# Right-hand sums of four weight quarters made in DRAM, and a new order of copies around the first relu

## The reference, cut to what matters

```python
def gmlp_mixer(h, w_in, ln_g, w_s, b_s, w_out):
    u, v = jnp.split(jax.nn.gelu(h @ w_in), 2, axis=-1)          # w_in 1024 x 4096
    v = layer_norm(v) * ln_g                                      # shortened here
    sv = jnp.einsum('gts,bnsge->bntge', tril(w_s), v) + b_s       # in chunks of 128 rows
    return (u * sv) @ w_out                                       # w_out 2048 x 1024

def channel_mlp(h, w1, w2):
    return jnp.square(jax.nn.relu(h @ w1)) @ w2                   # w1 1024 x 4096, w2 4096 x 1024

x = x + gmlp_mixer(rms_norm(x, norm1_g), ...)
x = x + channel_mlp(rms_norm(x, norm2_g), mlp_w1, mlp_w2)
return rms_norm(x, final_g)
```

## Time and profile before

| | |
|---|---|
| median of 3 runs | 1078.0 us (1076.59 to 1078.86) |
| the profiled execution, its own time | 1075.86 us |
| its span in the profile | 1073.6 us |
| PE busy | 1061.0 us (99%) |
| DVE busy | 795.4 us (74%) |
| ACT busy | 561.6 us (52%) |
| POOL busy | 43.9 us (4%) |
| transfers of SP's queue (q1) | 195.33 MB |
| transfers of POOL's queue (q0) | 9.96 MB |

### The profile page before, as it was taken

How to read it: one execution, slowest core, us unless ns; L and a number is a source line. 1 busy time by engine, 2 the same in 40 slices (tenths; PEclk the granted TensorE clock), 3 DMA queues, 4 the chain that set the end, 5 groups by cost and what they waited for, 6 DMA issues and landing times.

```text
span 1073.6 us, 13163 instructions
## 1 busy us (share of the span) xinstructions
PE 1061.0 (99%) x5050; PEld 929.5 (87%) x5050; DVE 795.4 (74%) x878; ACT 561.6 (52%) x875; POOL 43.9 (4%) x49
## 2 busy tenths in 40 slices
PE   9999999999999999999899999999999999999997
PEld 7888888888898888888788888888888888888886
DVE  5986656789789996899658548456599575777766
ACT  7864444553554434554774465454654434434456
POOL 0010000000000000111000000000000000000250
PEclk9999999999999999999999999999999999999999
DMA  9089873372875495755353734637888365343223
GB/s 337 17 188 320 230 228 113 103 249 86 323 275 220 170 349 193 198 167 158 134 180 118 229 124 172 215 108 265 323 300 341 113 236 200 118 155 121 79 79 157
DMA packets 86286, 206.39 MB, mean 192 GB/s; under 512 B 5400, under 2 KB 12592, under 8 KB 79024
## 3 DMA queue, kind: packets, MB, share of 16 engines
q1 hardware_dynamic: 82576, 195.33, 52.2%
q0 software_dynamic: 3488, 9.96, 3.8%
q10 hardware_dynamic: 160, 0.27, 0.1%
HBM read 143.67 MB, written 67.11 MB: 196 GB/s over the span
## 4 chain that ended last, share of the span: by engine, by line
PE 90%; DVE 5%; ACT 2%; issue 2%; POOL 0%; DMA 0%; DVEq 0%; ACTq 0%; POOLq 0%
PE banks L467 29%; PE banks L472 29%; PE banks L471 29%; PE banks L560 2%; PE banks L599 1%; DVE ring_low L1496 1%; DVE raw_a L1597 1%; DVE pair_low L1504 1%; DVE rows L1709 0%; DVE rows L1647 0%; ACT ring_high L1039 0%; POOL quad_a L408 0%; PE banks L567 0%; DVE rows L1474 0%; DVE raw_s L1630 0%
## 5 line engine op out<-in xcount | busy, mean ns | idle before, releaser
L1069 ACT ACTIVATE pair_high<-left_and_right 128x1024 fp32r<-128x1024 f32 x168 | 176.6, 1056 | 223.4 <-PE banks L467 186.7
L1496 DVE TENSOR_TENSOR ring_low<-left_and_right,ring_high 128x512 fp32r<-128x512 f32 x224 | 152.2, 692 | 165.4 <-ACT ring_high L1039 164.7
L1504 DVE TENSOR_TENSOR pair_low<-left_and_right,pair_high 128x1024 fp32r<-128x1024 f32 x168 | 204.2, 1232 | 85.2 <-ACT pair_high L1069 85.2
L467 PE MATMUL banks<-pair_high 128*128 128x512 f32 x672 | 255.0, 379 | 0.1
L471 PE MATMUL banks<-pair_low,pair_high 128*128 128x512 f32 x672 | 254.7, 379 | 0.0
L472 PE MATMUL banks<-pair_high,pair_low 128*128 128x512 f32 x672 | 254.7, 379 | 0.0
L1039 ACT ACTIVATE ring_high<-left_and_right 128x512 fp32r<-128x512 f32 x224 | 136.9, 627 | 219.5 <-PE banks L467 132.5
L467 PE MATMUL banks<-s_high,ring_high 128*128 128x512 f32 x384 | 146.5, 382 | 4.3 <-DVE s_low L1585 4.2
L472 PE MATMUL banks<-s_high,ring_low 128*128 128x512 f32 x384 | 146.3, 381 | 0.0
L471 PE MATMUL banks<-s_low,ring_high 128*128 128x512 f32 x384 | 146.2, 381 | 0.0
L467 PEld LDWEIGHTS banks<-pair_high 128*128 128x128 f32 x672 | 127.0, 189 | 18.4 <-DVE scratch L1694 0.5
(11 more groups left out here) (141 smaller groups left out, 1243.4 us busy)
## 6 DMA issues: line engine op xcount, KB each, us to landing
left_and_right<-sums SPq DMA_DIRECT2D x40, 1024.0 KB, 7.3
sums<-rows SPq DMA_DIRECT2D x34, 1024.0 KB, 5.2
left_and_right<-in_mlp_w_dram SPq DMA_DIRECT2D x34, 1024.0 KB, 7.2
left_and_right<-in_a_w_in_dram SPq DMA_DIRECT2D x19, 1024.0 KB, 8.4
v_blocks<-rows SPq DMA_DIRECT2D x8, 1024.0 KB, 7.9
left_and_right<-in_a_w_out_dram SPq DMA_DIRECT2D x8, 1024.0 KB, 10.5
rows<-in_x_dram SPq DMA_DIRECT2D x7, 1024.0 KB, 9.2
right_sums<-in_mlp_w_dram POOLq DMA_DIRECT2D x6, 1024.0 KB, 14.7
```

Source lines behind the costliest of these rows:

```text
L467: first = nc.tensor.matmul(ps[:, bank, :], stat_high, mov_high, start=start, stop=False, skip_group_check=True)
L1069: nc.scalar.activation(pair_high[pair_entry(d, pos, k)][:, :, :], pair_of(d, pos, k), ACT.Copy)\
L1496: nc.vector.tensor_tensor(ring_low[k][:, :], right_place(n, pos)[:, k, :], ring_high[k][:, :].bitcast(F32), ALU.subtract).then_inc(low_don ...
L1504: nc.vector.tensor_tensor(pair_low[e][:, :, :], pair_of(d, pos, k), pair_high[e][:, :, :].bitcast(F32), ALU.subtract).then_inc(low_done, 1)
```

## The change

POOL makes t1 to t4 in DRAM for n = 4, 5, 6 and 7, in one loop: each quarter's eight transfers start when the last ones of the quarter before have landed. `sum_t` is left out of DVE's stream for n = 5, 6, 7, and SP loads t1 to t4 of these quarters into the quarter buffers. For this it issues t3 and t1 ahead of the stores of the previous quarter's sums, t2 in the place of b12, and t4 in the place of the second load of b21. That makes seven loads of 1 MB for a quarter where there were five.

Around the first relu block of n = 4, ACT's stream is put in another order: `snap(4, 1)` ahead of the last two steps of s1, `high_combo(4, "s3")` and two splits of product 4 ahead of `activate(4, "c11")`. In DVE's stream `low_combo(4, "s3")` goes ahead of the splits of product 4. In quarters 2 and 3 one split of the next product (`next_low(n, 2)`) moves two operations ahead, into `gate(n, "c12")`. At the end the add of the last row block goes ahead of the scaling of the one before it.

```diff
-    return 4 * n + i + 1 + (4 if n > 4 else 0)
+    return 4 * n + i + 1
...
 def t_sum_double(d, i):
-    return (16 if d == 0 else 36 + 8 * (d - 1)) + i + 1
+    return 16 + 8 * d + i + 1
...
         scale_dram = nc.dram_tensor("row_scales", [MT, P], F32).ap()
-        t_dram = nc.dram_tensor("right_sums", [4, P, QT * NB], F32).ap()
+        t_dram = nc.dram_tensor("right_sums", [4, 4, P, QT * NB], F32).ap()
         y_dram = nc.dram_tensor("y_blocks", [4, NB, NB], F32).ap()
...
-        def t_of(t):
-            return t_dram[int(t[1]) - 1].rearrange("p (k s) -> p k s", s=NB)
+        def t_of(n, t):
+            return t_dram[n - 4, int(t[1]) - 1].rearrange("p (k s) -> p k s", s=NB)
...
-            def load_sum(t, b):
-                i = places(4)[b]
-                sp.wait_ge(t_made[t], 32)
-                load((t, 4), quarter[i][:, :, :], t_of(t), quarter_landed[i], f"quarter{i}")
+            def load_sum(n, t, b):
+                i = places(n)[b]
+                sp.wait_ge(t_made[t], 32 * (n - 3))
+                load((t, n), quarter[i][:, :, :], t_of(n, t), quarter_landed[i], f"quarter{i}")
...
                 previous_rest(prev)
+                if n > 4:
+                    sp.wait_ge(low_done, unit(n, 0, 3) + 1)
+                    load_sum(n, "t3", "b11")
+                if n >= 4:
+                    sp.wait_ge(low_done, unit(n, 1, 3) + 1)
+                    load_sum(n, "t1", "b21")
                 if prev in SUMMED:
                     store_s(prev, 0)
-                if prev in SUMMED:
                     store_s(prev, 1)
...
-                if n == 4:
-                    sp.wait_ge(low_done, unit(4, 1, 3) + 1)
-                    load_sum("t1", "b21")
                 sp.wait_ge(low_done, unit(n, 3, 3) + 1)
-                if n == 4:
-                    load_sum("t4", "b21")
+                if n >= 4:
+                    load_sum(n, "t4", "b21")
                 else:
...
                     load_weight(n + 1, "b11")
-                    if n != 4:
+                    if n < 4:
                         sp.wait_ge(t_summed, t_sum(n, 3))
-                    load_weight(n + 1, "b12")
+                        load_weight(n + 1, "b12")
+                    else:
+                        load_sum(n + 1, "t2", "b12")
                     sp.wait_ge(low_done, unit(n, 5, 3) + 1)
...
                     sp.wait_ge(low_done, unit_double(0, 6, 3) + 1)
-                    load_sum("t2", "b12")
+                    load_sum(4, "t2", "b12")
                     sp.wait_ge(low_done, unit_double(0, 6, 7) + 1)
...
                     sp.wait_ge(low_done, unit(4, 0, 3) + 1)
-                    load_sum("t3", "b11")
+                    load_sum(4, "t3", "b11")
                     sp.dma_start(y_of("c21"), block_of["c21"]).then_inc(y_stored["c21"], 16)
...
-                if n == 4 and pos in SUM_OF:
-                    act.wait_ge(*landed[SUM_OF[pos], 4])
+                if n >= 4 and pos in SUM_OF:
+                    act.wait_ge(*landed[SUM_OF[pos], n])
                 elif pos in (0, 1, 5):
...
             def right_place(n, pos):
-                return quarter[places(n)[(RIGHT_PLACE_SUMS if n == 4 else RIGHT_PLACE)[pos]]]
+                return quarter[places(n)[(RIGHT_PLACE_SUMS if n >= 4 else RIGHT_PLACE)[pos]]]
...
                     split_high(4, 3, 1)
-                    for k in range(1, 4):
-                        high_step(4, "s1", k)
+                    high_step(4, "s1", 1)
                     split_high(4, 3, 2)
+                    snap(4, 1)
+                    high_step(4, "s1", 2)
+                    high_step(4, "s1", 3)
                     split_high(4, 3, 3)
+                    high_combo(4, "s3")
+                    split_high(4, 4, 0)
+                    split_high(4, 4, 1)
                     activate(4, "c11")
...
-                if n > 0:
+                if n not in (0, 4):
                     split_high(n, 4, 0)
-                if n == 4:
-                    high_combo(4, "s3")
-                if n > 0:
                     split_high(n, 4, 1)
...
             def right_place(n, pos):
-                return quarter[places(n)[(RIGHT_PLACE_SUMS if n == 4 else RIGHT_PLACE)[pos]]]
+                return quarter[places(n)[(RIGHT_PLACE_SUMS if n >= 4 else RIGHT_PLACE)[pos]]]
...
                     args = q["b21"], q["b11"], q["b21"]
-                nc.vector.tensor_tensor(*args, ALU.subtract if n < 4 else ALU.add).then_inc(t_summed, 1)
+                nc.vector.tensor_tensor(*args, ALU.subtract).then_inc(t_summed, 1)
...
                 gate_sum(n, blk, 3)
+                if blk == "c12":
+                    next_low(n, 2)
                 gate_product(n, blk, 2)
...
                     split_low(n, 1, 0)
-                    sum_t(n, 0)
+                    if n < 4:
+                        sum_t(n, 0)
                     split_low(n, 1, 1)
...
                 if n != 4:
-                    sum_t(n, 1)
+                    if n < 4:
+                        sum_t(n, 1)
                     if n == 0:
...
                           .then_inc(drained[bank], 1)
-                if n not in (0, 4):
+                if 0 < n < 4:
                     sum_t(n, 2)
...
                     dve.wait_ge(bias_landed, 16)
+                if n == 4:
+                    low_combo(4, "s3")
                 split_low(n, 4, 0)
                 split_low(n, 4, 1)
-                if n == 4:
-                    low_combo(4, "s3")
                 if n == 0:
...
                 else:
-                    if n != 4:
+                    if n < 4:
                         sum_t(n, 3)
...
                     next_low(n, 1)
-                next_low(n, 2)
+                if kind(n) != "u":
+                    next_low(n, 2)
                 next_low(n, 3)
...
                 dve.wait_ge(o_step, m)
+                if i == 2:
+                    add_rows(2, 6, [3])
                 finish_a(m)
-                if i < 3:
+                if i < 2:
                     add_rows(2, 6, [i + 1])
...
                                     pattern=[[0, GROUPS], [-1, P]], channel_multiplier=1).then_inc(ws_masked, 1)
-            nc.gpsimd.dma_start(t_of("t1"), weight(4, "b11")).then_inc(t_made["t1"], 16)
-            nc.gpsimd.dma_start(t_of("t3"), weight(4, "b12")).then_inc(t_made["t3"], 16)
-            pool.wait_ge(t_made["t1"], 16)
-            nc.gpsimd.dma_start(t_of("t1"), weight(4, "b12"), accum_op=ALU.add).then_inc(t_made["t1"], 16)
-            pool.wait_ge(t_made["t3"], 16)
-            nc.gpsimd.dma_start(t_of("t3"), weight(4, "b22"), accum_op=ALU.add).then_inc(t_made["t3"], 16)
-            pool.wait_ge(t_made["t1"], 32)
-            nc.gpsimd.dma_start(t_of("t2"), t_of("t1")).then_inc(t_made["t2"], 16)
-            pool.wait_ge(t_made["t2"], 16)
-            nc.gpsimd.dma_start(t_of("t2"), weight(4, "b22"), accum_op=ALU.add).then_inc(t_made["t2"], 16)
-            pool.wait_ge(t_made["t2"], 32)
-            nc.gpsimd.dma_start(t_of("t4"), t_of("t2")).then_inc(t_made["t4"], 16)
-            pool.wait_ge(t_made["t4"], 16)
-            nc.gpsimd.dma_start(t_of("t4"), weight(4, "b21"), accum_op=ALU.add).then_inc(t_made["t4"], 16)
+            for n in range(4, 8):
+                before = 32 * (n - 4)
+                nc.gpsimd.dma_start(t_of(n, "t1"), weight(n, "b11")).then_inc(t_made["t1"], 16)
+                nc.gpsimd.dma_start(t_of(n, "t3"), weight(n, "b12")).then_inc(t_made["t3"], 16)
+                pool.wait_ge(t_made["t1"], before + 16)
+                nc.gpsimd.dma_start(t_of(n, "t1"), weight(n, "b12"), accum_op=ALU.add).then_inc(t_made["t1"], 16)
+                pool.wait_ge(t_made["t3"], before + 16)
+                nc.gpsimd.dma_start(t_of(n, "t3"), weight(n, "b22"), accum_op=ALU.add).then_inc(t_made["t3"], 16)
+                pool.wait_ge(t_made["t1"], before + 32)
+                nc.gpsimd.dma_start(t_of(n, "t2"), t_of(n, "t1")).then_inc(t_made["t2"], 16)
+                pool.wait_ge(t_made["t2"], before + 16)
+                nc.gpsimd.dma_start(t_of(n, "t2"), weight(n, "b22"), accum_op=ALU.add).then_inc(t_made["t2"], 16)
+                pool.wait_ge(t_made["t2"], before + 32)
+                nc.gpsimd.dma_start(t_of(n, "t4"), t_of(n, "t2")).then_inc(t_made["t4"], 16)
+                pool.wait_ge(t_made["t4"], before + 16)
+                nc.gpsimd.dma_start(t_of(n, "t4"), weight(n, "b21"), accum_op=ALU.add).then_inc(t_made["t4"], 16)
+                pool.wait_ge(t_made["t3"], before + 32)
+                pool.wait_ge(t_made["t4"], before + 32)
             y_final(pool, "c22")
...
             pool.wait_ge(low_done, unit_double(0, 5, 7) + 1)
```

## The result

The changed kernel takes 1090.37 us, the median of four runs (1089.63 to 1091.02), beside 1078.38 for four of the kernel before (1076.59 to 1078.86). The ratio is 1.0116, with a 95% interval of 1.010 to 1.0131: slower by 12 us, where +4.9 was forecast. The profiled execution took 1089.95 and its span is 1087.9, 14.3 longer than before.

A forecast was written before the change was run, and what follows sets the result against it. PE, at 99% busy, was taken to bound the kernel. Orders -5.0 and -0.5, store +4.6, loads +4.0 and clock +1.8 sum to +4.9 us: 1080.8 profiled, median 1082.9, range for 8 in 10 from 1071.5 to 1092.

The forecast's parts named there:

- What bounds the kernel: Whole kernel: PE busy 1061.0 of 1073.6 us, so only its stalls and low clock can be won; DVE's sums worth 0.
- The new order at n = 4: First relu block of n = 4: stall and low clock go, 6.0 us, less 1.0 for later steps; gain 5.0.
- The end: Last row block: its add starts about 0.5 us earlier, ahead of the previous block's scaling; gain 0.5, at most 0.75.
- POOL's transfers: Quarters 1 to 3: three more sets end between 290 and 352 us, one under way at 211 and at 267 to 287.
- The load of v's c22: Quarters 2 and 3: load 4.3 us late with 2.3 in hand; PE stalls 2.0 in each, 4.0 together.
- The store ahead of `snap(3, 1)` in quarter 3: SP's store lands 7 us late, bound 22, against a 2.4 margin at the small matmuls; PE stalls 4.6, clock adds 1.8.
- The sum: Whole kernel: -5.0 - 0.5 + 4.6 + 4.0 + 1.8 = +4.9 us; 1080.8 for the profiled execution, 1082.9 as median.
- the likeliest case: Whole kernel: the forecast itself, a slower kernel, chance 0.47, own range 1080.2 to 1090 us.
- Rival 3: Quarters 2 and 3: SP's queue backs up worse, store 15 us late, 12.6 of stall, 3 per load; 1094.7, chance 0.08.
- Rival 4: n = 4: the new order does not take the stall away, 5 us dearer than forecast; 1087.9, chance 0.05.
- 1: Rival, quarters 2 and 3: transfers hidden, stores under 2.4 us late and loads under 2.3; -5.5 remains, 1072.5, chance 0.29.
- 2: Rival, whole kernel: gains and losses cancel, stalls with their clock cost of 3.3 to 7.7 us; 1078, chance 0.11.

The follow-up runs named there:

- experiment 7: Changed kernel with the set for n = 5 straight behind n = 4, and n = 6 and 7 in quarters 4 and 5: 1071.12 us, ratio 0.995.
- experiment 1: Kernel before plus only the new orders and the moved split, without the sets for n = 5 to 7; DVE keeps its sums: 1070.26 us, ratio 0.9942.
- experiment 6: Changed kernel with the set for n = 5 moved to the first double, n = 6 and 7 to quarters 4 and 5: 1096.59 us, ratio 1.0178.
- experiment 2: Kernel before plus three further POOL sets behind that for n = 4, results unused: 1094.92 us, ratio 1.0172.
- experiment 4: Kernel before plus one unused POOL set held back to about 261 us: 1090.22 us, ratio 1.0125.
- experiment 5: As experiment 4, with the set's four adding transfers made plain copies of the same size: 1088.23 us, ratio 1.0106.
- experiment 8: Experiment 1 with `snap(4, 1)` behind the split of s3 and two splits of product 4, y's c21 squares behind the split of s4: 1070.54 us, ratio 0.9943.
- experiment 10: Experiment 8 run once more unchanged, against the kernel before: 1069.43 us, ratio 0.9926.

## Why the prediction was right in its sign and wrong in its size

- **What bounds the kernel.** Right: PE's standing still and its clock set the time, and DVE's 25 us off cost or gave nothing that shows (experiment 7 against 1).
- **The new order at n = 4.** -5.0 forecast, -5.4 measured in the changed kernel: the stall -4.4, the clock -1.8, the third step of s1 +0.54 for 0.5, product 5 +0.24 for 0.5. Right in each part.
- **The end.** -0.5 forecast, -0.39 measured.
- **POOL's transfers.** The sets end at 329.7, inside 290 to 352, and are under way at the places named. Right.
- **The load of v's c22.** Quarter 2: 2.0 forecast, 1.15 + 0.99 = 2.1 measured. Quarter 3: 2.0 forecast, 0.3 measured. In quarter 3 the load, issued at 317.33, landed in 7.6 us, 2.8 later than the 4.8 of before and not 4.3: POOL's queue had nothing to move until its last add, issued at 318.58, and had moved 0.5 MB when the load landed.
- **The store ahead of `snap(3, 1)` in quarter 3: this is the step that failed, and by its size.** I had written "less than half of the bound, and I take 7"; it was 12.9, and the bound of 22 held. I had argued that a set does not always move data, and that what is lost early is partly won back. Up to the store's issue it was not: 2.46 of the 4.19 MB in front of it were still to be moved, where before none were. SP's queue did get the engines to itself, but from 294.2 to 301.6 only, when the store had been waiting for 6 us. So it landed in 17.5 us for 5.5. The margin was off too: PE does not wait at the small matmuls (2.4) but earlier, at the banks of product 4 (1.8), which the same copy empties. Stall and clock came to 11.0 + 2.0 = 13.0 for 4.6 + 1.8 = 6.4.
- **A term left out:** the load of v's c21 for quarter 3, for which ACT waited 0.84 before. It came 9.5 late with nearly 7 in hand, and cost 2.7. Small steps that no term covers come to 1.6 (0.17, 0.62, 0.83).
- **The sum.** Forecast: +4.9. Measured in the profiled execution +14.1: 6.6 more for the store, 2.7 for c21, 1.6 small steps, -1.5 for c22, -0.3 for the orders and the end, which is 9.1 of the 9.2 between them. The medians differ by 12.0 and not 14.1; the executions of one kernel lie 1.4 us (experiment 1) to 8.5 us (experiment 6) apart. The median of 1090.37 is inside the range for 8 in 10 (1071.5 to 1092) and just above the likeliest case's own (1080.2 to 1090).
- **The rivals.** Rival 3 (the store late by 15, 1094.7) had the right mechanism and came nearer to the truth than the forecast in the stall, 12.6 for 11.0; at 0.08 it had too little. Rival 4 did not occur, and neither did 1 and 2: the transfers were not hidden, and they cost far more than the orders gained.

What stays open is how late the store would have been without the backlog in front of it, beside POOL's transfers alone. It was not tried with the store issued on another queue.

## What to carry to other kernels

Traffic that no engine waits for is not free: here it took its turns on the DMA engines, and its price was set by the loads and stores with the least margin in the stretch where it ran. Before it is placed, list for each transfer there how long its landing is ahead of its use, those without a wait too, and count a queue's backlog, not each transfer alone; then place it where the list is long. With one engine at 99%, taking work off another bought nothing here, and reordering one split ahead of a relu bought more than twelve operations removed.

## What the runs showed of the hardware that was not expected

- The store of 1 MB from SP took 5.5 us to land with POOL's queue idle, 13.6 beside the set of plain copies and 16.5 beside the set with adds, in both with a backlog of SP's own queue in front of it. Turns went by packets and not by bytes: 260 to 261 packets were 0.53 to 0.52 MB beside adds, 269 to 267 were 0.55 to 1.06 beside copies.
- POOL's copy from one place of `right_sums` to another went in sixteen packets of 64 KB, which took 2.4 us each by the trace. In the changed kernel they stood from 291.4 to 295.7, and in 292.5:294 SP's queue started only ten packets (0.02 MB).
- After a stall the clock's lower level cost PE between 1.6 and 3.1 us, not in step with the stall's length: 1.6 behind a wait of 2.35 (experiment 2), 1.8 behind the stall of 4.2 before and 2.9 behind the same one in experiment 4, 2.65 behind 6.2 (experiment 5), 2.8 behind 9.2 (experiment 4), 3.1 behind 9.4 (experiment 2), 2.0 behind 11.0. A short stall did not always bring it. Behind the wait at the small matmuls of c21, 2.35 us in experiment 2 and 2.40 in the changed kernel, the granted clock was 0.50 in the one and 1.00 in the other:
```profile
256.90:259.00 2.10, 2.08 (x9) 2.08 (x10) 1.58 (x2) 2.10 (x5) 0.00 (x0) 0.50 1.08 201
...
257.00:259.00 2.00, 1.98 (x17) 1.98 (x18) 1.48 (x2) 2.00 (x5) 0.00 (x0) 1.00 1.03 159
```
- Beside the one set that every version has, for n = 4, quarter 1 was longer by 0, 1.7 and 3.5 us in three profiled executions of nearly the same program (experiments 1, 8 and 10).
